# First attention with deeper probability slots, other quotient, square and rotary steps; two gate tiles moved; matmuls placed in waits

## The chip, the cores and the metric

The kernel runs on one core of one Trainium2 chip. The metric is the time of one execution in device microseconds (us). A core has a matmul engine (TensorE, PE in the profile; its weight loads are PEld), a vector engine (VectorE, DVE), an activation engine (ScalarE, ACT), GpSimd (POOL), a queue engine for transfers (SyncE, SP), a large on-chip memory (SBUF) and the matmuls' accumulators (PSUM, eight banks of 512 columns).

## What is computed

Two different two-layer blocks, one after the other, on a sequence of 512 rows of width 1024, in float32. A layer of the first block mixes three attentions behind one input projection:

```
proj = rms_norm(x, attn_norm[l]) @ w_in[l]
o_mla  = rms_norm(mla_attention(h_mla, ...), mla_out_norm[l])      # 6 heads, rotary on 32 of 96 columns
o_diff = diff_attention(h_diff, ...)                               # 6 heads, a = softmax_0 - lam * softmax_1, then rms_norm
o_ch   = rms_norm(chunk_attention(h_ch, ...), chunk_out_norm[l])   # 4 heads, relative bias
x = x + concatenate([o_mla, o_diff, o_ch]) @ w_out[l]
x = x + conv_ffn(rms_norm(x, ffn_norm[l]), ...)                    # width 2816, three-tap convolution
```

A layer of the second block has a banded attention (8 heads) and three dilated ones (12 heads) whose outputs are combined by their softmax denominators, two sigmoid gates, a projection, a layer norm, a squared-relu network of width 4096 with a gated extra term, and another layer norm:

```
ob = sum over g of softmax(lse)[g] * outs[g]
h = (sigmoid(gate_a) * (oa @ w_branch_a) + sigmoid(gate_b) * (ob @ w_branch_b)) @ w_out
x = layer_norm(alpha * x + h);  x = layer_norm(alpha * x + mlp(x) + ple(x))
```

## The kernel before, in words

Activations lie transposed, 128 of the 1024 features by 512 rows in a chunk. Every float32 weight is split into a high half and a remainder, and so is every activation: a product is three matmuls (L513, L514, L515) in the fast float32 form. A dense tile is 8 chunks by 3 matmuls, 24 in all. Weights come as 460 units of 128x1024. POOL issues the load of a unit's high half (L481) once PE has used up the slot, and then subtracts (L486, two SBUF inputs) to get the remainder. The tiles' PSUM banks go round a ring, banks 2 and 3 alone during the attentions, and `d_free` tells PE that a bank has been read.

**First attention** (`attention_1`, 64 tasks a layer). A task is one head and one block of 128 query rows. Diff tasks have two score maps, the others one. Tasks 0 to 7 are diff, 8 to 15 chunk, 16 to 31 diff, 32 to 55 mla, 56 to 63 chunk. PE's iteration `it` issues the score matmuls of task it+1 (L691; three PSUM banks go round, so the second map of a diff task waits for the reduction of the first map of the task before), then a piece of other work (`fill`: quarters of dense tiles up to iteration 23, from 24 to 36 the mla's small products), then the transposes of task it-2 (L704) and the value matmuls of task it-3 (L714). DVE's iteration `it` reduces the scores of task it to negated logits and a minimum (L1075), after a wait until the transposes of the slot's last user are done: six slots go round by map, so that for diff tasks the last user is three tasks back. Then it forms the quotient of the two denominators of task it-1 (L1085, L1086) and the difference of the maps (L1088), the reciprocal that scales the output (L1090), scales the output of task it-4 out of PSUM (L1095, `on_ready`: frees the bank for PE's L704), squares and sums the output of task it-5 (L1102, both inputs in SBUF), and runs `side(it)`: evacuation of finished dense tiles (L1062), norm factors, and the rotary step of one tile, four dependent instructions (L1206 to L1209). ACT takes the exponentials (L1640), copies transposed probabilities to SBUF (L1647) and evacuates.

After the attention the outputs are scaled by their norm factors, turned into chunks (L727) and split.

**Second attention** (`attention`, 80 tasks). PE's fill is 12 rotary tiles and 12 gate tiles in 96 quarters, spread over the 80 iterations by `pieces`. Then the rows of minima and denominators are turned (L921), 4 more gate tiles run while DVE forms the combination's weights, the weights are spread over partitions by six matmuls whose moving operand has four rows (L930), DVE combines (L1500 to L1502), and PE waits for the last split chunk of the result (L934) before the branch products.

**Norms behind a row.** `factor_from_row` (L869) waits for ACT's root of a row (L1609), turns the row into columns (L874), waits for DVE's reciprocal (L1406) and spreads the factor (L576). PE then waits for the first split chunk of the normalized activations. It runs once after the first block and once in each of the four layer norms, the last of which ends the kernel. In the residual before the first of them DVE sums the squares in `rx`, in SBUF (L1015, L1018).

## Time and profile before

| | |
|---|---|
| median of 3 runs (range) | 3231.89 us (3230.84 to 3237.18) |
| the profiled execution | 3240.42 us, span 3238.7 us |
| mean granted TensorE clock | 0.964 of 2.4 GHz |
| PE busy | 3112.6 us, 96% of the span |
| DVE, ACT, POOL busy | 41%, 25%, 42% |
| first attention, layer 0 and 1 | 60.8 to 306.4 us, 771.3 to 1011.9 us |
| second attention, layer 0 and 1 | 1510 to 1772 us, 2408 to 2670 us |

A timeline row gives start, duration, engine, line, operation, output and inputs, and in brackets how long the engine had been idle and who released it. Several matmul instructions in one row are given as xN; a plain float32 matmul counts as two. Matmuls are pipelined, so the time from start to start is their price, not the duration of one. The granted clock of a stretch is 1.00 at 2.4 GHz and 0.50 at 1.2 GHz.

### The profile page before, as it was taken

The page shows a single profiled execution, that of the slowest core. Times are in us where ns is not written, and L with a number is a line of the kernel's source. Part 1 is how long each engine was busy: PE and PEld are TensorE (multiplying, and loading weights), DVE is VectorE, ACT ScalarE, POOL GpSimd, SP SyncE. Part 2 cuts the span into 40 slices and gives each one's busy share as a digit, 9 for nine tenths or more (in the row PEclk, how much of TensorE's full clock was granted, in tenths as well). Part 3 has the DMA queues.
Part 4 walks back from the last instruction along what each step waited for, and adds up shares of the span by engine and source line. Part 5 has one row for each costly group of instructions (what it writes and reads, how often), then busy time and mean ns, then how long its engine had stood idle before and what let it go on. Part 6 is the DMA issues. An engine that isn't in the chain of part 4 may idle for free.

```text
span 3238.7 us, 40314 instructions
## 1 busy us (share of the span) xinstructions
PE 3112.6 (96%) x13950; PEld 2448.0 (76%) x13950; DVE 1324.1 (41%) x2953; ACT 809.4 (25%) x1811; POOL 1363.7 (42%) x924
## 2 busy tenths in 40 slices
PE   7989999999899999999999999999999999999998
PEld 6767788888667788878666778888686667788886
DVE  5476434244574534353630741112337307411113
ACT  3345212122244212121333221101213333210112
POOL 4211555564211555554222445555352234455552
PEclk9888999999879999999999999999999999999999
DMA  6211566664222566655233556566452235456663
GB/s 239 91 53 53 183 194 194 192 214 153 91 65 79 180 194 187 201 177 176 84 97 112 158 167 193 189 189 202 130 182 91 89 113 157 155 189 189 206 192 102
DMA packets 136518, 494.06 MB, mean 153 GB/s; under 512 B 15280, under 2 KB 15536, under 8 KB 136112
## 3 DMA queue, kind: packets, MB, share of 16 engines
q0 software_dynamic: 66240, 241.20, 24.2%
q1 hardware_dynamic: 68544, 245.40, 23.3%
q10 hardware_dynamic: 1584, 5.40, 0.5%
q8 instruction: 102, 1.67, 0.2%
q14 instruction: 48, 0.39, 0.0%
HBM read 489.84 MB, written 2.10 MB: 152 GB/s over the span
## 4 chain that ended last, share of the span: by engine, by line
PE 91%; DVE 4%; issue 2%; ACT 1%; DMA 1%; POOL 0%; DVEq 0%; SPq 0%; POOLq 0%; ACTq 0%
PE ps L513 25%; PE ps L514 24%; PE ps L515 24%; PE ps L744 3%; PE ps L769 3%; PE ps L691 3%; PE ps L714 2%; PE ps L640 1%; PE ps L641 1%; PE ps L642 1%; PE ps L704 1%; PE ps L757 1%; PE ps L902 1%; DVE small L1086 1%; PE ps L921 0%
## 5 line engine op out<-in xcount | busy, mean ns | idle before, releaser
L513 PE MATMUL ps<-hi,w_hi 128*128 128x512 f32 x3216 | 1294.1, 402 | 34.2 <-POOL w_lo L486 15.2
L514 PE MATMUL ps<-hi,w_lo 128*128 128x512 f32 x3216 | 1268.1, 394 | 0.0
L515 PE MATMUL ps<-lo,w_hi 128*128 128x512 f32 x3216 | 1266.7, 394 | 0.0
L486 POOL TENSOR_TENSOR w_lo<-w_raw,w_hi 128x1024 fp32r<-128x1024 f32 x460 | 1105.8, 2404 | 104.8 <-DMA w_hi<-weights 95.3
L481 POOL DMA_DIRECT2D w_hi<-weights x460 | 261.4, 568 | 1728.2 <-PE ps L515 1573.6
L513 PEld LDWEIGHTS ps<-hi,w_hi 128*128 128x128 f32 x3216 | 612.5, 190 | 233.6 <-issue 94.9
L515 PEld LDWEIGHTS ps<-lo,w_hi 128*128 128x128 f32 x3216 | 612.9, 191 | 131.7
L514 PEld LDWEIGHTS ps<-hi,w_lo 128*128 128x128 f32 x3216 | 613.8, 191 | 121.0
L1120 DVE CUSTOM_DVE_ANT_0 pr<-ps,kc 128x128 f32<-128x128 f32 (+2 forms) x160 | 65.3, 408 | 340.8 <-PE ps L744 340.8
L1803 ACT ACTIVATE ps<-hb,col 128x512 f32<-128x512 f32 x88 | 68.5, 782 | 381.1 <-DVE hb L1062 381.1
L1538 DVE SCALAR_TENSOR_TENSOR x<-x,ps 128x512 f32<-128x512 f32 x64 | 43.9, 687 | 287.1 <-PE ps L515 287.1
L1898 ACT ACTIVATE sq<-ps 128x512 f32<-128x512 f32 x64 | 38.2, 597 | 469.4 <-PE ps L515 469.4
L1671 ACT ACTIVATE pT<-ps 128x128 f32<-128x128 f32 (+2 forms) x160 | 59.8, 374 | 311.6 <-PE ps L757 311.6
L1215 DVE TENSOR_TENSOR x<-x,ps 128x512 f32<-128x512 f32 x64 | 43.8, 687 | 227.5 <-PE ps L515 227.5
L1062 DVE TENSOR_TENSOR hb<-ps,rx 128x512 f32<-128x512 f32 x88 | 60.1, 686 | 187.3 <-PE ps L515 174.3
L1532 DVE SCALAR_TENSOR_TENSOR ps<-ps,sq 128x512 f32<-128x512 f32 x64 | 44.7, 698 | 216.5 <-ACT sq L1898 147.4
L993 DVE TENSOR_TENSOR lo<-ps,hi 128x512 fp32r<-128x512 f32 x108 | 74.7, 692 | 77.1 <-ACT hi L1571 77.1
L769 PE MATMUL ps<-pT,v 128*64 128x128 f32 x608 | 100.7, 286 | 0.3
L640 PE MATMUL ps<-w_hi,hi 128*128 128x384 f32 (+2 forms) x256 | 87.3, 341 | 2.7 <-issue 2.0
L769 PEld LDWEIGHTS ps<-pT,v 128*64 128x64 f32 x608 | 62.0, 136 | 34.3 <-issue 33.1
L1571 ACT ACTIVATE hi<-ps 128x512 fp32r<-128x512 f32 x108 | 64.7, 599 | 88.0 <-DVE ps L1532 54.5
L642 PE MATMUL ps<-w_hi,lo 128*128 128x384 f32 (+2 forms) x256 | 86.4, 337 | 0.0
(317 smaller groups left out, 3235.5 us busy)
## 6 DMA issues: line engine op xcount, KB each, us to landing
w_raw<-weights SPq DMA_DIRECT2D x460, 512.0 KB, 3.8
w_hi<-weights POOLq DMA_DIRECT2D x460, 512.0 KB, 4.5
x<-xt SPq DMA_DIRECT2D x8, 256.0 KB, 10.4
out<-x SPq DMA_DIRECT2D x8, 256.0 KB, 2.1
kc<-k ACTq DMA_DIRECT2D x1, 1281.0 KB, 5.8
bias<-relb ACTq DMA_DIRECT2D x2, 512.0 KB, 5.4
bias<-relb ACTq DMA_DIRECT2D x1, 1024.0 KB, 5.0
praw<-pt ACTq DMA_DIRECT2D x2, 512.0 KB, 3.6
```

The source lines that it names most:

```text
L481: pool.dma_start(whi[s][:, :], weights[i * RING + s]).then_inc(w_hi_in[s], 16)
L486: nc.gpsimd.tensor_tensor(wlo[s][:, :], raw[s][:, :], whi[s][:, :].bitcast(F32), ALU.subtract).then_inc(w_split, 1)
L513: nc.tensor.matmul(out_ap, w[0], xx[0], start=first, stop=False)
L514: nc.tensor.matmul(out_ap, w[1], xx[0], start=False, stop=False)
L515: return nc.tensor.matmul(out_ap, w[0], xx[1], start=False, stop=last)
L640: nc.tensor.matmul(o, xh, whi[slot][:, w], start=(u == 0 and k == 0), stop=False)
L642: last = nc.tensor.matmul(o, xl, whi[slot][:, w], start=False, stop=(u == n_units - 1 and k == per - 1))
L691: nc.tensor.matmul(ps[:, S_BANK[q.s % 3], 0:t.n], lq, rk, start=True, stop=True).then_inc(s_done, 1)
L744: nc.tensor.matmul(ps[:, S_BANK[q.s % 3], 0:t.n], lq, rk, start=True, stop=True).then_inc(s_done, 1)
L769: last = nc.tensor.matmul(ps[t.base:t.base + 64, O_BANK, t.qb * P:(t.qb + 1) * P], v, slots(it - 3)[1][t.id % 2][:, kb * P:(kb + 1) * P], ...
L993: V.tensor_tensor(dst[1][:, i, :], src, dst[0][:, i, :].bitcast(F32), ALU.subtract).then_inc(lo_ready, 1)
L1803: A_(cv[k], hb[k][:, 2:S + 2], ACT.Identity, bias=pcol("conv", l, 3 * 44 + j), scale=pcol("conv", l, 2 * 44 + j)).then_inc(act_step, 1)
```

## The change

In the first attention a probability map goes to slot `task % 4`, the second map of a diff task to slot 4 or 5. DVE's reduction waits for the transposes of the task four back, or, for a second map, for its own difference two diff tasks back. The scale of the quotient becomes a tensor_scalar with two per-row scalars. The reciprocals are kept in a tile of 64 columns. The square pass reads the unscaled output in PSUM and the scaled one in SBUF, writes its product to PSUM, runs in the same iteration as the scaling (with a wait between them), and `on_ready` now follows it; the missing factor is put in by one multiplication before the norm factors. The rotary step of a tile is cut in two, the second half one iteration later. In the last residual of the first block the squares are summed in PSUM. In the second attention two gate tiles leave the fill (88 quarters) and stand behind L930. `keep_busy` adds plain float32 matmuls of 512 columns into bank 2: three at the start, two before PE's wait for the row's root and two after the spread of the factor.

```diff
-                            if s - 6 in SLOT_TASK:
-                                dve.wait_ge(t_done, SLOT_TASK[s - 6] + 1)
+                            if m:
+                                if q.pair >= 2:
+                                    dve.wait_ge(p_ready, t.p0 - 1)
+                                q.pair += 1
+                            elif it >= 4:
+                                dve.wait_ge(t_done, t.id - 3)
...
-                            link(V.scalar_tensor_tensor(out=quot(s), in0=quot(s + 1), scalar=lam, in1=rsum(s), op0=ALU.mult,
-                                                        op1=ALU.mult))
-                            V.scalar_tensor_tensor(out=p0, in0=pb[(s + 1) % 6][:, 0:t.n], scalar=quot(s), in1=p0,
+                            link(V.tensor_scalar(quot(s), quot(s + 1), lam, rsum(s), ALU.mult, ALU.mult))
+                            V.scalar_tensor_tensor(out=p0, in0=p1, scalar=quot(s), in1=p0,
                                                    op0=ALU.mult, op1=ALU.add).then_inc(p_ready, 1)
-                        V.reciprocal(rinv(on0 + it - 1), rsum(s)).then_inc(rinv_ready, 1)
...
-                        V.tensor_scalar(t.more["out"], ps[:, TO_BANK[i % 3], 0:64], rinv(on0 + i), None,
-                                        ALU.mult).then_inc(on_ready, 1)
-                    if 0 <= it - 5 < n:
...
-                        V.tensor_tensor_reduce(out=junk[:, :], in0=t.more["out"], in1=t.more["out"], scale=1.0, scalar=0.0,
-                                               op0=ALU.mult, op1=ALU.add, accum_out=t.more["ss"]).then_inc(ss_ready, 1)
+                        link(V.tensor_scalar(t.more["out"], ps[:, TO_BANK[i % 3], 0:64], rinv(t.more["ss"]), None, ALU.mult))
+                    if 1 <= it <= n:
+                        t = ts[it - 1]
+                        V.reciprocal(rinv(t.more["ss"]), rsum(t.s0)).then_inc(rinv_ready, 1)
+                    if 0 <= it - 4 < n:
+                        if on0 + it - 4:
+                            dve.wait_ge(on_ready, on0 + it - 4)
+                        V.tensor_tensor_reduce(out=ps[:, TO_BANK[i % 3], 64:128], in0=ps[:, TO_BANK[i % 3], 0:64], in1=ts[i].more["out"], scale=1.0,
+                                               scalar=0.0, op0=ALU.mult, op1=ALU.add,
+                                               accum_out=ss[:, ts[i].more["ss"]:ts[i].more["ss"] + 1]).then_inc(on_ready, 1)
...
-                to, so_far = (rx[:, :] if n < NC_ or c == n - 1 else acc), (rx[:, :] if n < NC_ else acc)
+                to, so_far = (rx[:, :] if n < NC_ - 1 or c == n - 1 else acc), (rx[:, :] if n < NC_ - 1 else acc)
...
-        N_ROPE, N_GATE, N_CHAIN = 12, 12, 4
+        N_ROPE, N_GATE, N_CHAIN, N_COMBINE = 12, 10, 4, 2
...
+            def keep_busy(n, rows):
+                for _ in range(n):
+                    nc.tensor.matmul(ps[:, 2, :], ident, rows, start=True, stop=True)
+
             pe.wait_ge(par_in, 48)
+            keep_busy(3, kc1[:, 0:S])
...
             def factor_from_row():
+                keep_busy(2, kc2[:, K2["cos"]:K2["cos"] + S])
                 q.root += 1
                 pe.wait_ge(row_rooted, q.root)
...
                 q.norm += 1
+                keep_busy(2, kc2[:, K2["cos"]:K2["cos"] + S])
...
                                          bk[g][0:4, :], start=True, stop=True).then_inc(wbc, 1)
+                quarters(4 * N_COMBINE, A)
                 oneed = q.chunk
...
+                    if it == AT_KR + 1:
+                        rope_96_add(kr)
+                    elif ITEM_AT.get(it - 3, " ")[0] == "Q":
+                        rope_96_add(mq[b][int(ITEM_AT[it - 3][1])])
...
+                        link(V.tensor_tensor(ss[:, 0:48], ss[:, 0:48], rinvs[:, 0:48], ALU.mult))
...
-                for j in range(N_GATE, 2 * NC_):
+                for j in range(N_GATE, N_GATE + N_CHAIN):
                     gate(j)
                 for pair in range(2):
                     q.val += 1
                     act.wait_ge(val_ready, q.val)
                     high(tmp[pair][:, :], (ohi, olo), 4 + pair)
+                    gate(N_GATE + N_CHAIN + pair)
```

## Rows read from the trace of the kernel before

**Rows 1.** The page, part 4: shares by engine of the chain that ended last.

```profile
PE 91%; DVE 4%; issue 2%; ACT 1%; DMA 1%; POOL 0%; DVEq 0%; SPq 0%; POOLq 0%; ACTq 0%
```

**Rows 2.** Windows, attentions: length, busy PE PEld DVE ACT POOL, clock, DMA, GB/s.

```profile
60.84:306.40 245.56, 223.34 (x1041) 167.53 (x1041) 161.95 (x582) 101.55 (x278) 46.05 (x31) 0.86 0.22 71
771.27:1011.90 240.63, 224.04 (x1041) 167.11 (x1041) 152.62 (x572) 98.41 (x274) 45.87 (x31) 0.86 0.24 73
1518.00:1772.00 254.00, 253.87 (x1175) 173.66 (x1173) 107.80 (x339) 86.92 (x287) 69.47 (x48) 1.00 0.30 96
```

**Rows 3.** PE's waits, first attention of layer 0: us in total, times, longest.

```profile
PE ps L691 <- DVE small L1075: 11.6, 5, 4.3
PE ps L576 <- DVE tmp L1062: 2.0, 1, 2.0
```

**Rows 4.** PE's waits, first attention of layer 1, same columns.

```profile
PE ps L691 <- DVE small L1075: 7.5, 5, 2.9
```

**Rows 5.** Timeline of layer 0's first attention: DVE, POOL and PE.

```profile
177.92 0.29 DVE L1075 CUSTOM_DVE_ANT_0 mk<-ps,dist 128x128 f32<-128x128 f32 x1 [3.43 <-PE ps L704]
178.54 2.68 DVE L1086 SCALAR_TENSOR_TENSOR small<-small 128x1 f32<-128x1 f32 x1
178.79 2.41 POOL L486 TENSOR_TENSOR w_lo<-w_raw,w_hi 128x1024 fp32r<-128x1024 f32 x1
...
185.11 0.68 DVE L1209 TENSOR_TENSOR tmp<-tmp,tmp 32x512 f32<-32x512 f32 x1
186.31 1.48 PE L691 MATMUL ps<-dk,dq 32*128 32x384 f32 x2 [2.79 <-DVE small L1075]
```

**Rows 6.** Lines L1086, L1102, L1088, whole run: ns min/median/max, first and last start.

```profile
L1086 DVE SCALAR_TENSOR_TENSOR small<-small x48: 218/220/2901, 64.6 to 944.5; 128x1 f32<-128x1 f32 x48
L1102 DVE CUSTOM_DVE_ANT_0 junk<-vd x48: 211/215/2385, 187.5 to 975.0; 128x64 f32<-128x64 f32 x48
L1088 DVE SCALAR_TENSOR_TENSOR mk<-mk,small,mk x23: 351/484/752, 64.9 to 912.5; 128x128 f32<-128x128 f32 x7, 128x256 f32<-128x256 f32 x6, 128x512 f32<-128x512 f32 x6, 128x384 f32<-128x384 f32 x4
```

**Rows 7.** Timeline of DVE: a square pass in layer 0.

```profile
148.35 2.49 DVE L1102 CUSTOM_DVE_ANT_0 junk<-dq 128x64 f32<-128x64 f32 x1
```

**Rows 8.** Windows behind gaps, columns as Rows 2: one stretch, sum of eight.

```profile
186.80:193.60 6.80, 6.80 (x18) 4.62 (x17) 0.88 (x6) 0.59 (x4) 0.00 (x0) 0.52 0.00 0
...
sum 47.70, PE 46.16 PEld 32.33 DVE 21.46 ACT 9.54 POOL 0.08; mean PE 5.77 PEld 4.04 DVE 2.68 ACT 1.19 POOL 0.01
```

**Rows 9.** Timeline, combination of the second block's layer 0: PE; then the window.

```profile
1803.07 5.91 PE L930 MATMUL ps<-bk,kc 4*128 4x512 f32 x12
1813.08 0.80 PE L513 MATMUL ps<-ohi,w_hi 128*128 128x512 f32 x1 [4.11 <-DVE olo L993]
...
1808.10:1818.30 10.20, 6.09 (x15) 4.11 (x14) 4.69 (x8) 3.69 (x5) 0.00 (x0) 0.51 0.11 45
```

**Rows 10.** Timeline and window, layer norm of the second block's layer 0: PE.

```profile
1896.32 7.03 PE L902 MATMUL ps<-sq,kc 128*1 128x512 f32 x16 [1.51 <-ACT sq L1583]
1904.11 1.05 PE L874 MATMUL ps<-kc,tmp 1*128 1x1 f32 x8 [0.77 <-ACT tmp L1609]
1909.07 0.77 PE L513 MATMUL ps<-hi,w_hi 128*128 128x512 f32 x1 [2.47 <-DVE lo L1440]
...
1907.00:1914.00 7.00, 4.93 (x12) 3.94 (x13) 6.73 (x11) 6.44 (x10) 0.00 (x0) 0.52 0.01 2
```

**Rows 11.** Timeline and windows, norm after the first block: PE; line L1018.

```profile
1432.95 1.05 PE L874 MATMUL ps<-kc,tmp 1*128 1x1 f32 x8 [2.11 <-ACT tmp L1609]
...
1436.00:1443.00 7.00, 5.25 (x13) 4.17 (x14) 6.82 (x11) 3.58 (x6) 0.00 (x0) 0.53 0.00 0
...
L1018 DVE TENSOR_TENSOR rx<-rx,sq x5: 1046/1622/2254, 1411.5 to 1427.8; 128x512 f32<-128x512 f32 x5
```

**Rows 12.** The start: ACT's and PE's first rows, then two windows, PE alone.

```profile
9.91 1.33 ACT L1597 ACTIVATE hi<-x,col 128x512 fp32r<-128x512 f32 x2 [3.97 <-DMA col<-cols]
...
14.97 0.77 PE L513 MATMUL ps<-hi,w_hi 128*128 128x512 f32 x1 [14.97 <-POOL w_lo L486]
...
15.00:19.00 4.00, 4.00 (x10) 1.00 1.04 408
19.00:28.00 9.00, 9.00 (x41) 1.00 0.99 362
```

More of the change, by code:

```diff
@@ L108, in __init__ @@
         self.s = self.task = self.o = self.x = self.rope = self.kcopy = self.bca = self.bcd = self.mu = 0
-        self.sink = self.on = self.chunks = self.root = self.mean = self.back = self.sd = self.var = self.sums = self.aux = self.quarter = 0
+        self.sink = self.on = self.chunks = self.root = self.mean = self.back = self.sd = self.var = self.sums = self.aux = self.quarter = self.pair = 0
     def freed(self, bank):
@@ L253, in build @@
         rsum = lambda s: small[:, 32 + s % 16:33 + s % 16]
-        rinv = lambda s: small[:, 48 + s % 16:49 + s % 16]
+        rinv2 = lambda s: small[:, 48 + s % 16:49 + s % 16]
+        rinv = lambda k: rinvs[:, k:k + 1]
         esk = lambda s: small[:, 64 + s % 16:65 + s % 16]
@@ L364, in tasks_1 @@
                                   0, None, qb, False, False, add=dist[:, off:off + n], after=after,
-                                  out=dn[h // 2][:, qb, 64 * (h % 2):64 * (h % 2) + 64], ss=ss[:, 4 * h + qb:4 * h + qb + 1]))
+                                  out=dn[h // 2][:, qb, 64 * (h % 2):64 * (h % 2) + 64], ss=4 * h + qb))
             for h in range(CH_H):
@@ L384, in tasks_1 @@
                                    out=mn[h // 2][:, qb, 64 * (h % 2):64 * (h % 2) + 64],
-                                   ss=ss[:, 24 + 6 * qb + h:25 + 6 * qb + h], value=tile_1(l, f"V{qb}") if h == 0 else None, **more))
+                                   ss=24 + 6 * qb + h, value=tile_1(l, f"V{qb}") if h == 0 else None, **more))
             return d[0:8] + c_[0:8] + d[8:24] + m_ + c_[8:16]
@@ L704, in attention_1 @@
                             last = nc.tensor.transpose(ps[:, TO_BANK[i % 3], kb * P:(kb + 1) * P],
-                                                       slots(i)[0][t.s0 % 6][:, kb * P:(kb + 1) * P], ident)
+                                                       slots(i)[0][i % 4][:, kb * P:(kb + 1) * P], ident)
                         last.then_inc(t_done, 1)
@@ L1066, in attention_1 @@
                 on0 = q.on
-                for it in range(n + 5):
+                for it in range(n + 4):
                     if it < n:
@@ L1072, in attention_1 @@
                             dve.wait_ge(s_done, s + 1)
[L1073 to L1076 removed]
+                            if m:
[4 more added lines that the diff above has]
+                                dve.wait_ge(t_done, t.id - 3)
+                            V.tensor_tensor_reduce(out=pb[4 + it % 2 if m else it % 4][:, 0:t.n], in0=ps[:, S_BANK[s % 3], 0:t.n],
+                                                   in1=t.more["add"], scale=-t.scale, scalar=3.0e38, op0=ALU.add, op1=ALU.min,
                                                    accum_out=ngm(s)).then_inc(s_free, 1)
@@ L1133, in attention @@
                         p0 = pb[s % 6][:, 0:t.n]
-                        if t.kind == "diff":
-                            V.reciprocal(rinv(s), rsum(s))
-                            link(V.reciprocal(rinv(s + 1), rsum(s + 1)))
-                            V.tensor_scalar(p0, p0, rinv(s), None, ALU.mult)
-                            link(V.tensor_scalar(rinv(s + 1), rinv(s + 1), lam, None, ALU.mult))
-                            V.scalar_tensor_tensor(out=p0, in0=pb[(s + 1) % 6][:, 0:t.n], scalar=rinv(s + 1), in1=p0,
-                                                   op0=ALU.mult, op1=ALU.add).then_inc(p_ready, 1)
-                        elif t.kind in ("norm", "sink"):
-                            if t.kind == "sink":
-                                link(V.tensor_tensor(rsum(s), rsum(s), esk(s), ALU.add))
-                            link(V.reciprocal(rinv(s), rsum(s)))
-                            V.tensor_scalar(p0, p0, rinv(s), None, ALU.mult).then_inc(p_ready, 1)
+                        if t.kind == "sink":
+                            link(V.tensor_tensor(rsum(s), rsum(s), esk(s), ALU.add))
+                            link(V.reciprocal(rinv2(s), rsum(s)))
+                            V.tensor_scalar(p0, p0, rinv2(s), None, ALU.mult).then_inc(p_ready, 1)
                     if side:
@@ L1317, in side @@
                         dve.wait_ge(*landed(name))
-                        rope_96(mq[b][int(name[1])])
+                        rope_96_turn(mq[b][int(name[1])])
                     elif it == AT_FACTOR:
-                        dve.wait_ge(ss_ready, q.on + 56)
+                        dve.wait_ge(on_ready, q.on + 56)
+                        link(V.tensor_tensor(ss[:, 0:48], ss[:, 0:48], rinvs[:, 0:48], ALU.mult))
                         link(V.reduce_sum(ss[:, 24:28], ss[:, 24:48].rearrange("p (q h) -> p q h", q=NTB), axis=AX.X))
@@ L1356, in low_turned @@
                     q.chunk += 1
-                dve.wait_ge(ss_ready, q.on)
+                dve.wait_ge(on_ready, q.on)
+                link(V.tensor_tensor(ss[:, 48:64], ss[:, 48:64], rinvs[:, 48:64], ALU.mult))
                 link(V.reduce_sum(ss[:, 48:52], ss[:, 48:64].rearrange("p (q h) -> p q h", q=NTB), axis=AX.X))
@@ L1474, in _ @@
                 attention(TASKS["2", l], slots_2, side=dilated)
-                q.tile += N_GATE + N_CHAIN
-                q.unit += N_GATE + N_CHAIN
+                q.tile += N_GATE + N_CHAIN + N_COMBINE
+                q.unit += N_GATE + N_CHAIN + N_COMBINE
                 for c in range(4):
```

24 lines of the change are left out of this document (10 added, 14 removed).

## The prediction

> **What bounds the kernel now.** I read the chain of waits first: PE carries 91% of it and DVE 4% [rows 1], so the time is PE's own work, its idle gaps, and the stretches in which it works at half clock. Then the windows, for where that is. The first attention takes 245.6 and 240.6 us, PE is idle for 22 and 17 us of them, and the granted clock is 0.86; the second attention is idle for 0.1 us of 254 at 1.00 [rows 2]. PE's waits in the first attention name mostly one releaser, the score reductions L1075: 11.6 us in layer 0, 7.5 in layer 1, and beside them one wait of 2.0 us in each layer for an evacuation L1062 [rows 3, 4].
>
> The timeline shows how such a gap comes about [rows 5]. DVE idles 3.43 us until PE's transposes free a slot (177.92). Its quotient L1086, 0.22 us in the median, then takes 2.68 us while POOL's subtraction L486 runs. Evacuation and four rotary instructions follow, and PE, whose next score matmul needs the next reduction, idles 2.79 us until 186.31. Then it works at 1.2 GHz: from 186.8 to 193.6 the clock is 0.52 with PE busy throughout [rows 8]. I compared the clock with the gaps one by one: each low stretch of the first attention stands at or just behind a gap of PE. So a gap is paid twice, as idle time and as half-speed work behind it.
>
> **The change, part by part**, against the profiled execution (span 3238.7, its time 3240.4).
>
> *Slots.* For a diff task the wait for transposes goes from three tasks back to four. Three back, it could be met only after PE's fill and transposes of the iteration whose scores are already there. Four back, it is met before those scores are issued. DVE now reduces beside the fill, some 3 us earlier, and that much delay no longer reaches PE. Single-map tasks fall from six slots to four at no cost, by the same order. Behind a second map's new wait nothing is queued that its own difference, two diff tasks back, hasn't passed.
>
> *Quotient and square.* L1086 and L1102 go from 0.22 us to 2.9 and 2.5 when they meet POOL [rows 6, 7]. The new square pass has one SBUF input, and I cost it at the 0.22 us of the old. L1088 still has two SBUF inputs. It never took over 0.75 us [rows 6], but it always stood behind L1086, which had sat out POOL's instruction, so that row doesn't excuse it. I expect that it mostly misses POOL now, because with the new slots the quotient runs beside the fill, and POOL starts when a fill's last quarter frees a unit.
>
> The Trainium skill, "SBUF — State Buffer", section "Who interferes with whom", says that a DVE instruction with two SBUF inputs contends with a GpSimd instruction that reads SBUF, that the one that comes second is blocked for the whole instruction, and that a DVE instruction with at most one SBUF input outside the two-port modes isn't. By that rule L1102's stalls go, while L1086's may only move on to L1088; that result is the second case below. The trace agrees for the two lines that it shows stalled.
>
> *Rotary in halves.* The same four instructions, some 0.7 us each, in two iterations: a block of 2.8 us becomes two of 1.4. The halves end one iteration later, with three or more iterations to go before their tasks.
>
> *What is late next.* In iterations 24 to 36 DVE is as full as PE (diff tasks plus six rotary tiles), so I count nothing there. The 4.3 us gap of layer 0 comes from the rotary angles, a chain of instructions the change doesn't touch. What is open are the gaps 1.27, 2.79, 1.31 and 2.0 us in layer 0 and 1.30, 2.86, 0.94 and 2.0 in layer 1, 14.5 us, and the eight low stretches behind them, in which PE is busy for 46.2 us [rows 8] that full clock would do in half: 23.1. Together 37.6 us. Others that stay (1.3 us for ACT's squares, 0.8 for an evacuation) will keep some stretches low, so I take two thirds, 25. Bounds: 10 (only the two 2.0 us gaps, which a square pass causes, with half of their low stretches' work) and 41.
>
> *Later `on_ready`.* PE's transposes and the turn of the outputs now wait for the square too, about 0.35 us behind the scaling (the square with its accumulator read, 0.30, and the wait). Inside the attention the slack of an iteration hides it. At its end, with one more small multiplication, I charge 0.6 us a layer: -1.2. Attention: **-24**.
>
> *Sums of squares in PSUM.* The last L1018 takes 1.05 us [rows 11] and is waited for; the PSUM form elsewhere takes 0.70. **-0.35**.
>
> *Start.* The parameters are there at 9.9, PE starts at 14.97, and its first ten matmuls take 0.40 us each against 0.22 later [rows 12] (the clock column says 1.00 there, the spacing says half). Three `keep_busy` matmuls at half speed take 3 x 1.76 = 5.3 us and end at 15.2. The ten then save 1.8 us, and the load of the next high half, issued when these tiles end, comes as much earlier: **-1.8** (bounds 0 and -2).
>
> *Norms.* A plain matmul of 512 columns is 7.03/8 = 0.88 us [rows 10], a pair 1.76. In the norm after the first block the wait for the root is 2.11 us [rows 11], so the first pair hides. In the layer norms that wait is 0.77 us [rows 10], and the pair overhangs by 1.0 us, four times. The pair after the spread hides (2.3 to 2.5 us of idle time). What it can bring is the clock: 0.52 for 7 us behind each norm [rows 10, 11]. PE's busy time there is 4.9 and 5.25 us, half of which is the loss, capped by DVE's chunks, which come every 1.4 to 1.5 us: 2.2 us a layer norm, 2.9 the first. I believe in a kept clock at 0.75 for three layer norms and 0.65 for the first: 1.9 + 3 x (1.65 - 1.0) - 1.0 for the last, after which PE has nothing to do = **-3** (bounds +4 and -5.7).
>
> *Two gate tiles.* Each is 24 matmuls at 0.228 us, 5.5. They leave an attention without idle time, which gets shorter by 10.9 us, and stand where PE now idles 4.11 us [rows 9]. They end at about 1819, after DVE's last chunk, which becomes ready at about 1816 since its ACT half is now queued behind a gate evacuation that waits for the first tile. So the 4.1 us go whole; the sigmoids start some 5 us later and have the branch tiles' four banks as cover. The clock is already low as L930 ends, before the gap begins (low from 1808.1), so I don't expect it to stay up: 6.1 us busy at half [rows 9] become 3.4 to 7. I take 4.5 a layer, **-9** (bounds -6 and -13).
>
> Sum: 24 + 0.35 + 1.8 + 3 + 9 = 38.2 us. The profiled execution is 8.5 us above the runs' median; from the median 3231.9 the forecast is **3193.7 us**.
>
> **The rivals.** *Forecast*, 3183 to 3203, chance 0.50.
>
> *The stall moves on.* L1088 meets POOL in L1086's place. For it: its two inputs; against it: the new phase. Attention brings 10 - 1.2, the rest 14.2: 3209. Chance 0.24.
>
> *All gaps close* and every low stretch behind them: attention 40, norms 5.7, gates 13, start 2: 3171. Chance 0.16. Against it: gaps that belong to ACT and to the angles.
>
> *It doesn't do what it says*: DVE, busy for 162 of 246 us [rows 2], finds other waits (for the exponentials, for `pv_done`), the norms cost their 4 us, and the gates' gain is all that is left with it: 3228. Chance 0.06.
>
> *Slower.* The second attention loses 8 of 96 quarters, the densest work in it. If its clock then fell as in the first, from 1.00 to 0.86, each layer would take 254/0.86 - 254 = 41 us more: 3231.9 - 38 + 82 = 3276. It decides from a mean clock of 0.93, where 19 us a layer eat the gain. Against it: already now four of five iterations have one quarter, and none of the stretches between is low. Chance 0.04.
>
> **How the numbers follow.** The likeliest gives 3193.7. From 3172 to 3214 hold all of the forecast, most of the second case and half of the third, 0.8. 0.2% is 6.5 us, about what a measurement can tell. Faster by more: 0.50 + 0.24 + 0.16 and a little of the fourth, 0.91; the same 0.05; slower 0.04.
>
> **What would show it.** PE's waits for L1075 in the first attention under 8 us in both layers together (now 19.1) and its clock above 0.90; no instruction of the square pass above 0.4 us; L1088 at 2.4 us or more would be the second case. No wait of PE before the branch products; gate tiles at 1.2 GHz for part of their time. Between L902 and L874 some 1.8 us instead of 0.77, and full clock behind the norms. PE's first dense matmuls 0.22 us apart. Wrong it would be if the first attention took over 238 us in both layers, or if the second's clock left 1.00.

## The result, and the profile after

The changed kernel takes 3181.24 us (median of 5, 3175.22 to 3236.52); the kernel before, in the same session, 3231.89 (median of 5, 3220.64 to 3237.18). The medians are 50.6 us apart, where 38.2 were forecast. The ratio is 0.9837, with a 95% interval of 0.9816 to 0.9859; it leaves out executions over 1.5% above their kernel's fastest, here the one of 3236.52. A second set of four executions gave 3198.8 (3168.55 to 3236.9) against 3235.61, ratio 0.9888 (0.9834 to 0.9942).

The executions of the changed kernel lie 68 us apart, those of the old one 25. Two of the nine took 3236.52 and 3236.9 us, with mean clocks of 0.958 and 0.960. The first of them was profiled with the result: its clock stays low through the end of both first attentions. The rows below are from an execution of 3168.55 us (span 3166.9, after_again) unless a sentence says otherwise. That is the fastest of the nine, and the profiled execution of the kernel before (3240.42 us) is one of the longer ones: their spans differ by 71.8 us and not by 50.6, so what follows for each part is the gain between these two executions. The difference between the two kinds turned out to be the part of the result that I had not seen coming; tail_kick, below, is about it.

The chain of waits of the changed kernel, shares by engine (before: [rows 1]):

```profile
PE 93%; DVE 3%; issue 1%; ACT 1%; DMA 0%; POOL 0%; ACTq 0%; DVEq 0%; POOLq 0%
```

The two first attentions and a stretch of the second, columns as in [rows 2]:

```profile
58.73:282.39 223.66, 208.12 (x1042) 155.96 (x1042) 152.62 (x589) 100.78 (x278) 46.24 (x31) 0.90 0.25 80
745.28:958.25 212.97, 201.47 (x1041) 151.74 (x1041) 144.81 (x577) 96.98 (x274) 46.16 (x31) 0.93 0.27 84
1461.80:1695.00 233.20, 233.20 (x1086) 158.51 (x1084) 103.31 (x330) 82.12 (x272) 61.87 (x42) 1.00 0.30 92
```

The first attentions are 21.9 and 27.7 us shorter. PE's busy time fell by 15 and 23 us although it does the same matmuls: that is work done at full instead of half clock. The second attention keeps its 1.00, so the slower rival is out.

PE's waits in the first attention of layer 0, then of layer 1 (before: [rows 3, 4]):

```profile
PE ps L692 <- DVE small L1089: 5.2, 2, 4.3
PE ps L514 <- ACT mk L1770: 2.2, 2, 2.0
PE ps L692 <- ACT vc L1644: 1.8, 1, 1.8
...
PE ps L692 <- DVE small L1089: 1.2, 2, 0.9
```

The waits for a reduction (L1089, before L1075) fell from 11.6 and 7.5 us to 5.2 and 1.2. What is left is the 4.3 us of the rotary angles, and a wait for ACT's copy of K2 (L1770), one of the mla's small products.

The lines on DVE that answer to [rows 6]: the difference of the maps L1101, the quotient's scale L1100, the square pass L1114; ns min/median/max:

```profile
L1101 DVE SCALAR_TENSOR_TENSOR mk<-mq,small,mk x34: 352/619/3210, 62.8 to 865.9; 128x128 f32<-128x128 f32 x10, 128x256 f32<-128x256 f32 x8, 128x384 f32<-128x384 f32 x8, 128x512 f32<-128x512 f32 x8
L1100 DVE TENSOR_SCALAR small<-small x48: 272/273/276, 62.5 to 892.1; 128x1 f32<-128x1 f32 x48
L1114 DVE CUSTOM_DVE_ANT_0 ps<-ps,vd x48: 211/214/219, 170.3 to 920.0; 128x64 f32<-128x64 f32 x48
L1114 DVE CUSTOM_DVE_ANT_0 ps<-ps,vm x32: 212/214/233, 244.9 to 943.1; 128x64 f32<-128x64 f32 x32
```

The quotient and the square never stall any more, and not for want of meeting POOL: 4 of the 48 quotients and 18 of the 128 squares begin during one of its subtractions and take no longer than the others. The difference, which before never took over 0.75 us, now does: six of its 48 take over 1 us, two of these 3.21 and 2.77. The stall moved on, but to far fewer places.

The spread of the combination's weights (before: [rows 9]), and a window of the gate tiles:

```profile
1732.45 8.20 PE L939 MATMUL ps<-bk,kc 4*128 4x512 f32 x12
1740.58 0.79 PE L514 MATMUL ps<-hi,w_hi 128*128 128x512 f32 x1
1741.17 0.63 PE L515 MATMUL ps<-hi,w_lo 128*128 128x512 f32 x1
...
1736.00:1746.00 10.00, 10.00 (x20) 5.60 (x19) 5.67 (x9) 0.63 (x1) 0.03 (x1) 0.54 0.17 58
```

The 4.11 us of idle time before the branch products are gone. The first ten matmuls of the moved tiles stand 0.43 us apart, which is half clock; after that 0.23. The spread itself takes 8.20 us in this execution where L930 took 5.91, because the clock falls earlier in it (0.65 over it, before 0.90).

The norm of a layer norm, layer 0 (before: [rows 10]), and the window behind it:

```profile
1834.92 7.03 PE L911 MATMUL ps<-sq,kc 128*1 128x512 f32 x16 [1.51 <-ACT sq L1598]
1841.88 1.99 PE L780 MATMUL ps<-kc,kc 128*128 128x512 f32 x4
1843.79 1.05 PE L882 MATMUL ps<-kc,tmp 1*128 1x1 f32 x8
1845.12 1.16 PE L577 MATMUL ps<-kc,small 128*128 128x128 f32 x8 [0.28 <-DVE small L1421]
1846.11 1.88 PE L780 MATMUL ps<-kc,kc 128*128 128x512 f32 x4
1848.75 0.47 PE L514 MATMUL ps<-hi,w_hi 128*128 128x512 f32 x1 [0.76 <-DVE lo L1455]
...
1849.00:1856.00 7.00, 7.00 (x31) 5.08 (x31) 6.82 (x11) 6.68 (x12) 0.00 (x0) 1.00 0.00 0
```

From the squares' sum (L911) to the turn (L882) it is 8.87 us instead of 7.79 (L902 to L874): the pair overhangs by 1.1. The clock behind is 1.00 instead of 0.52.

The start (before: [rows 12]), PE, then its first window:

```profile
9.98 5.11 PE L780 MATMUL ps<-kc 128*128 128x512 f32 x6 [9.98 <-DMA col<-cols]
14.57 0.75 PE L514 MATMUL ps<-hi,w_hi 128*128 128x512 f32 x1
15.16 0.39 PE L515 MATMUL ps<-hi,w_lo 128*128 128x512 f32 x1
...
15.00:19.00 4.00, 4.00 (x19) 1.00 1.05 409
```

From 15 to 19 us PE starts 19 matmuls instead of 10.

I cut both traces at the same instructions and added up length, PE's idle time and time at half clock, in us:

| part | before | after |
|---|---|---|
| start | 60.8 / 17.4 / 0 | 58.7 / 12.5 / 0 |
| first attention, layer 0, iterations 0 to 23 | 142.6 / 12.5 / 37.5 | 129.0 / 7.2 / 23.9 |
| iterations 24 to 36 | 51.0 / 8.9 / 13.3 | 43.5 / 4.5 / 8.5 |
| iterations 37 to the end | 52.4 / 1.2 / 18.2 | 51.1 / 3.9 / 10.2 |
| layer 1, iterations 0 to 23 | 135.0 / 8.8 / 27.3 | 118.2 / 3.0 / 10.2 |
| iterations 24 to 36 | 52.0 / 6.0 / 20.9 | 43.6 / 4.7 / 8.5 |
| iterations 37 to the end | 53.7 / 1.9 / 19.5 | 51.2 / 3.9 / 10.2 |
| rest of the first block, with its last norm | 962.8 / 23.3 / 20.2 | 958.4 / 17.7 / 13.9 |
| second attention with its branch products, up to the layer norm, layer 0 | 382.4 / 5.5 / 20.4 | 377.6 / 1.5 / 13.6 |
| the same, layer 1 | 382.7 / 5.5 / 20.4 | 372.5 / 1.4 / 3.4 |
| layer norms and networks, four parts (idle time up to PE's last instruction) | 963.2 / 25.7 / 34.8 | 963.1 / 18.0 / 12.1 |

### The profile page after: what moved, and what is told of

Same layout as the page of the kernel before. It is cut to its first block, busy times and chain, and to the rows that moved or that the text cites. A ratio compares the mean times of both kernels' runs of the same rounds, so it can differ in the third digit from the quotient of the medians.

```text
span 3234.8 us, 40285 instructions
## 1 busy us (share of the span) xinstructions
PE 3153.1 (97%) x13996; PEld 2468.6 (76%) x13996; DVE 1305.9 (40%) x2957; ACT 808.3 (25%) x1811; POOL 1363.4 (42%) x924
## 3 DMA queue, kind: packets, MB, share of 16 engines
q1 hardware_dynamic: 68544, 245.40, 23.5%
## 4 chain that ended last, share of the span: by engine, by line
PE 93%; DVE 3%; issue 1%; ACT 1%; DMA 1%; POOL 0%; ACTq 0%; DVEq 0%; POOLq 0%
PE ps L514 25%; PE ps L515 24%; PE ps L516 23%; PE ps L692 3%; PE ps L745 3%; PE ps L770 3%; PE ps L715 3%; PE ps L705 2%; PE ps L641 1%; PE ps L643 1%; PE ps L642 1%; PE ps L758 1%; PE ps L911 1%; DMA w_hi<-weights 1%; PE ps L930 0%
## 5 line engine op out<-in xcount | busy, mean ns | idle before, releaser
L1914 ACT ACTIVATE sq<-ps 128x512 f32<-128x512 f32 x64 | 38.2, 597 | 465.8 <-PE ps L516 465.8
```

## Experiments

Each run's time stands beside the kernel before on the same chip (3233.6 to 3235.6 us). The first four ran together on one chip, the next four on a second, the last four on a third.

**after_again** is the changed kernel itself.

> The changed kernel as it is, for an undisturbed trace: about 3181 us. In the first attention PE's waits for the score reductions fall from 19.1 us in both layers to under 8, the clock rises above 0.90. If instead the stall only moved from the quotient to the difference of the maps, that line shows instructions of 2.4 us and the waits stay above 12 us.

Measured: 3198.8 us, ratio 0.9888 (0.9834 to 0.9942), and the trace above. The gain is there, but four executions from 3168.55 to 3236.9 can't tell a few us. I therefore read the other experiments by their traces' parts first and by medians second.

**old_slots** puts the old wait back and leaves the rest.

```diff
-                            elif it >= 4:
+                            if s - 6 in SLOT_TASK:
+                                dve.wait_ge(t_done, SLOT_TASK[s - 6] + 1)
+                            if not m and it >= 4:
                                 dve.wait_ge(t_done, t.id - 3)
```

> Only the slot wait is put back: a reduction of a diff task waits again for the transposes three tasks back. Theory 1 (the earlier reductions give PE its gain): some 22 us slower than the changed kernel, 3203 us, with waits of PE for the reductions of 10 us or more. Theory 2 (the passes that no longer wait for POOL give it): at most 5 us slower, 3186.

Measured: 3219.3 us, ratio 0.9946 (0.9923 to 0.9970). PE waits 9.6 and 5.8 us for reductions again. That is theory 1, with a time 16 us above the one that it gave. The first attentions take 246.3 and 240.1 us, together 486.4; before it was 486.6. By parts it is less even: iterations 0 to 36 take 187.9 and 177.2 us, 5.7 and 9.8 less than before and 15.4 more than in the changed kernel, in both layers; the end takes 58.4 and 62.9 us, with 20 and 28 of them at half clock, and gives the rest back. So the slots carry 15.4 of the 21.1 and 25.2 us that these iterations gained. The difference L1103 and DVE around one of its stalls, then POOL beside it:

```profile
L1103 DVE SCALAR_TENSOR_TENSOR mk<-mq,small,mk x34: 350/619/3139, 63.1 to 903.0; 128x128 f32<-128x128 f32 x10, 128x256 f32<-128x256 f32 x8, 128x384 f32<-128x384 f32 x8, 128x512 f32<-128x512 f32 x8
...
173.76 0.29 DVE L1091 CUSTOM_DVE_ANT_0 mk<-ps,dist 128x128 f32<-128x128 f32 x1 [3.20 <-issue]
174.39 0.27 DVE L1102 TENSOR_SCALAR small<-small 128x1 f32<-128x1 f32 x1
174.70 2.90 DVE L1103 SCALAR_TENSOR_TENSOR mk<-mq,small,mk 128x512 f32<-128x512 f32 x1
...
174.63 2.41 POOL L487 TENSOR_TENSOR w_lo<-w_raw,w_hi 128x1024 fp32r<-128x1024 f32 x1
```

This is the picture of [rows 5], one instruction later: DVE idles 3.20 us, passes the quotient in 0.27, and the difference sits out POOL's subtraction, which began 0.07 us earlier. It happens to 13 of the 48 differences, 1.8 to 3.1 us each, as it happened to 13 of 48 quotients in the old kernel. The new form of the quotient is not the one that is held up: in this run five quotients begin during a subtraction and take 0.27 us each, where all six that did so in the kernel before took 1.6 to 2.4. The rule of the Trainium skill ("SBUF — State Buffer", section "Who interferes with whom"), that a DVE instruction with two SBUF inputs contends with GpSimd's and that the one that comes second is blocked, is borne out by the line that took the stall over: all 11 differences that begin during a subtraction take 1.8 us or more. Which comes second can't be told by the recorded starts, though: 7 of the 13 quotients stalled in the kernel before began 0.24 to 0.47 us ahead of the subtraction, as the one of [rows 5] did. What takes the stall away is the phase: with the new slots 13 become 6, and of these only two exceed 1.3 us. How much of the 15.4 us is this, and how much the earlier reduction by itself, no run separates.

**old_lock** is the other half: new slots, but the quotient's scale and the square pass with two SBUF inputs as before.

```diff
-                            link(V.tensor_scalar(quot(s), quot(s + 1), lam, rsum(s), ALU.mult, ALU.mult))
+                            link(V.scalar_tensor_tensor(out=quot(s), in0=quot(s + 1), scalar=lam, in1=rsum(s), op0=ALU.mult,
+                                                        op1=ALU.mult))
...
-  in0=ps[:, TO_BANK[i % 3], 0:64], in1=ts[i].more["out"], scale=1.0,
+  in0=ts[i].more["out"], in1=ts[i].more["out"], scale=1.0,
```

> Only the quotient and the square pass read two SBUF inputs again. Theory 1 (slots): the square passes stall again, the two waits of 2.0 us at the spread and the low stretches behind them come back, some 8 us slower, 3189. Theory 2 (POOL's lock): 20 us slower, 3201.

Measured: 3199.32 us (3194.17 to 3201.88), ratio 0.9884 (0.9855 to 0.9914). Quotient, difference and square:

```profile
L1100 DVE SCALAR_TENSOR_TENSOR small<-small x48: 219/220/2681, 62.1 to 917.6; 128x1 f32<-128x1 f32 x48
L1102 DVE SCALAR_TENSOR_TENSOR mk<-mq,small,mk x34: 350/485/753, 62.4 to 891.8; 128x128 f32<-128x128 f32 x10, 128x256 f32<-128x256 f32 x8, 128x384 f32<-128x384 f32 x8, 128x512 f32<-128x512 f32 x8
L1115 DVE CUSTOM_DVE_ANT_0 ps<-vd x48: 213/215/2893, 170.0 to 953.8; 128x64 f32<-128x64 f32 x48
```

The quotient stalls three times (5.1 us together) where it stalled 13 times before. The square, now in the iteration of the scaling, stalls 22 times of 128, 52.7 us together, where it stalled 12 times (26.4 us). PE's wait for an evacuation before a spread, 2.0 us in the kernel before and gone in the changed one, is back too, 2.06 us in each layer, with 6.8 us at half clock behind it. In layer 0:

```profile
PE ps L577 <- DVE tmp L1072: 2.1, 1, 2.1
```

As a time, 3199.32 can't be told from the changed kernel's 3198.8. The first attentions take 239.4 and 232.9 us. In iterations 0 to 36 that is 1.7 and 8.1 us more than in the changed kernel; the rest, 14.1 and 11.8, lies in the end, at half clock for 41 and 36 us. So before the end of the attention the new forms of quotient and square together earn 1.7 and 8.1 us between these traces, of which some may be chance: two executions of the changed kernel differ by 4.6 us in iterations 0 to 23 alone (129.0 and 124.4). Whether the stalls at the end also bring the low clock there, or it was chance, these four executions don't say.

**gates_in_fill** puts the two gate tiles back into the attention.

```diff
-        N_ROPE, N_GATE, N_CHAIN, N_COMBINE = 12, 10, 4, 2
+        N_ROPE, N_GATE, N_CHAIN, N_COMBINE = 12, 12, 4, 0
```

> The two gate tiles go back into the fill of the second attention. Theory 1: PE idles 4.1 us again before the branch products in each layer and the clock stays low longer, 9 us slower, 3190. Rival (the clock is not low any more behind the gates): 13 us slower. Rival (the later sigmoids cost what the idle time gave): within 2 us.

Measured: 3200.21 us (3179.57 to 3217.12), which can't be told from 3198.8. PE's wait before the branch products is back:

```profile
PE ps L514 <- DVE olo L1003: 4.0, 1, 4.0
```

From the start of the second attention to the layer norm it takes 382.8 and 380.7 us. In the changed kernel that part varies by where the low stretches fall, so I took all eleven traces with the tiles moved: layer 0 from 372.6 to 379.1, mean 377.3; layer 1 from 372.5 to 379.7, mean 376.6. The three traces with the tiles in the fill (before, before_kick and this one) have a mean of 381.6. The move is worth 4.2 and 4.9 us, about the idle time it fills and no more.

**tail_kick** asks why executions of the same kernel lie 68 us apart. I compared the part from the end of the 2.0-us wait for K2 to the end of the attention. First the long execution (3236.5 us), then the short (3168.55), both layers each:

```profile
226.80:308.82 82.02, 80.60 (x280) 61.38 (x279) 39.93 (x192) 32.30 (x90) 8.25 (x5) 0.50 0.15 49
936.70:1018.83 82.13, 79.54 (x281) 60.94 (x281) 39.90 (x193) 32.43 (x91) 8.51 (x6) 0.52 0.15 49
...
231.10:282.39 51.29, 47.42 (x283) 37.11 (x282) 38.51 (x193) 32.35 (x91) 8.53 (x6) 0.90 0.24 79
906.98:958.25 51.27, 47.41 (x282) 37.09 (x281) 38.36 (x193) 32.31 (x91) 8.48 (x6) 0.90 0.23 79
```

The same matmuls, 82 us against 51: 61.6 of the 68 us between the two spans lie here. The engine that does the work isn't waiting (PE busy 80.6 of 82.0); in layer 0 it runs at 1.2 GHz from the wait on, to the end of the attention. In layer 1 the low clock that lasts doesn't begin behind the wait for K2. There the clock comes back, and falls for good at PE's next gap, in iteration 38, where PE waits for an exponential (L1655):

```profile
934.79 0.42 PE L514 MATMUL ps<-w_hi,mhi 128*128 128x384 f32 x1 [1.96 <-ACT mk L1770]
941.62 0.31 PE L705 MATMUL ps<-kc,pr 128*128 128x128 f32 x1 [1.01 <-ACT pr L1655]
...
935.70:939.10 3.40, 3.40 (x15) 2.69 (x13) 3.30 (x8) 1.37 (x4) 2.88 (x3) 0.50 0.50 148
939.10:942.50 3.40, 1.81 (x8) 0.82 (x7) 3.27 (x15) 1.58 (x5) 3.13 (x3) 1.00 0.67 213
942.60:1018.80 76.20, 75.25 (x265) 58.33 (x265) 34.14 (x175) 29.68 (x83) 2.90 (x3) 0.50 0.11 36
```

So it is in layer 1 of gates_in_fill and of no_root_pair, where a low stretch of 37.5 us begins at the same gap and the end takes 69.1 and 69.5 us. The short execution has the same gap (1.15 us) with no low clock behind it. The experiment puts four plain matmuls of 512 columns, from here on the kick, into iteration 39, just behind this gap, all else as in the changed kernel.

```diff
                     elif it in ITEM_AT:
                         item(ITEM_AT[it])
+                    elif it == 39:
+                        for bk_ in (2, 3):
+                            pe.wait_ge(d_free[bk_], q.freed(bk_))
+                        keep_busy(4, kc1[:, 0:S])
```

> The changed kernel with four plain matmuls of 512 columns at iteration 39 of each first attention, behind the wait for the last small product. Theory 1 (a low clock that begins with PE's last gap there outlasts the iterations without fill in some executions, and this makes the slow ones): the four cost 3.5 us a layer at full clock, the slow executions of 3199 us and more go, the spread between runs halves, the median falls to some 3178. Theory 2 (the clock of that part has nothing to do with what PE is given there): 7 us slower and as wide a spread.

Measured: 3185.0 us (3183.33 to 3190.05, five executions), ratio 0.9843 (0.9826 to 0.9861). The added matmuls and the same part of both layers:

```profile
238.94 3.60 PE L780 MATMUL ps<-kc 128*128 128x512 f32 x8
...
231.80:286.53 54.73, 50.93 (x290) 38.68 (x289) 38.68 (x192) 32.16 (x91) 8.50 (x6) 0.91 0.23 74
910.90:968.63 57.73, 53.58 (x290) 39.98 (x290) 38.29 (x192) 32.14 (x91) 8.54 (x6) 0.85 0.21 70
```

It costs 3.4 and 6.5 us against the short execution and saves 27 and 24 against the long one. With the kick, in this and three later kernels, 19 executions lie between 3178.2 and 3193.4. Without it 11 of 27 were over 3200 (five kernels: this one as it is, gates_in_fill, values_swapped, no_root_pair, rotary_whole); on the chip of tail_kick itself 5 of 14. The spread is what theory 1 said; the median is not, it stays at 3185.0 where some 3178 were expected.

**before_kick** asks whether the old kernel pays for the same thing: the same insertion in the kernel before.

> The kernel before, with the four plain matmuls of the run tail_kick (iteration 39 of each first attention, behind a wait for banks 2 and 3). Question: does the old kernel also lose time to a low clock in the iterations without fill? In its trace the low stretch behind the 2.0-us gap ended after 13.7 us of PE's work, in the changed kernel's slower executions it lasted 85 to 92 us. Theory A, the long low stretch belongs to the changed kernel alone (its tail is as dense as before, but PE has fewer gaps in front of it): the kick has nothing to remove, costs up to 2 x 3.5 us (four matmuls of 0.88 us) less what the gap hides, and the time is 3234 to 3243 beside the kernel before's 3235.6. Theory B, the old kernel pays for it in part of its executions as well: the time is 3215 to 3230, and part of what tail_kick brought isn't the change's.

Measured: 3235.54 us (3229.72 to 3250.65, 12 executions) against 3233.64, ratio 1.0017 (1.0001 to 1.0032). As a time the kick only costs. In its trace the two ends do get shorter, 51.2 and 51.3 us with 5.3 and 5.8 at half clock, where the old kernel's trace has 52.4 and 53.7 with 18.2 and 19.5, but not by enough to pay for it. Two ends of 82 us fit none of the old kernel's executions, which all lie within 25 us. So the long low stretch is new with the change.

What in the change lets it last is not shown. The work is the same, and nearly the same wait stands in front (2.2 us before, 2.0 after). One thing differs: the old kernel has no gap over 0.5 us between that wait and iteration 62, in either trace, and the changed one has those of iteration 38, 1.0 to 1.2 us and 0.6 behind it, in three of the four ends of its two traces. No run tests them alone. rotary_whole, below, has none of them and no execution over 3193.56, which would fit, but it is four executions; and in layer 0 of the long execution the low clock began before iteration 38.

**values_swapped** moves the wait for K2, by computing V2 ahead of it.

```diff
-"Q4", "Q5", "K2", "V2", "V3"]
+"Q4", "Q5", "V2", "K2", "V3"]
```

> The last two small products before the iterations without fill are V2 and K2 in the other order, so that V3 waits for a bank whose evacuation is one ACT instruction and not two. Theory: PE's gap of 2.0 us there shrinks below 1 and the low stretch behind it is shorter, 4 to 10 us in the median. Rival (the gap only moves to another product): within 3 us.

Measured: 3208.69 us (3171.65 to 3237.48), ratio 0.9898 (0.9860 to 0.9936). In its trace iterations 24 to 36 take 42.4 instead of 43.5 us, but the end 55.2 instead of 51.1: the wait shrank to 1.1 us, and the gap in iteration 38 grew to 1.67. Inconclusive as a time, and a no for the idea.

**rotary_whole** does the four rotary instructions in one iteration again.

```diff
-V.tensor_tensor(tmp[2][R, :], tmp[2][R, :], sin1[R, :], ALU.mult).then_inc(rope_turned, 1)
+V.tensor_tensor(tmp[2][R, :], tmp[2][R, :], sin1[R, :], ALU.mult)
+                link(V.tensor_tensor(t[R, :], t[R, :], cos1[R, :], ALU.mult))
+                V.tensor_tensor(t[R, :], t[R, :], tmp[2][R, :], ALU.add).then_inc(rope_done, 1)
```

> Only the rotary step is one piece again. Theory (the earlier reductions already cover the block of 2.8 us): within 4 us of the changed kernel, PE's waits for reductions longer by at most 2 us. Rival (the halves matter): such waits of 1.4 us and more come back at the rotary iterations, with low clock behind them, 10 us slower.

Measured: 3180.82 us (3177.76 to 3193.56), ratio 0.9846 (0.9820 to 0.9871), the lowest median of all. In the trace iterations 24 to 36 take 46.4 us instead of 43.5, and the end 48.9 instead of 51.1. The wait that the rival named does come back, 2.24 and 2.35 us in iteration 29, with low clock, and PE waits 7.5 and 3.4 us for reductions instead of 5.2 and 1.2. In return the gap in iteration 38 is gone. The halves shift 2.9 us out of one part and 2.2 us come back in the next: this piece of the change is worth nothing measurable.

**no_root_pair** leaves out the pair before the root in the four layer norms.

```diff
-                keep_busy(2, kc2[:, K2["cos"]:K2["cos"] + S])
+                if q.root == 0:
+                    keep_busy(2, kc2[:, K2["cos"]:K2["cos"] + S])
                 q.root += 1
```

> The pair of matmuls before the wait for the row's root is left out in the four layer norms and kept in the first norm. Theory: the root's columns (L874 of before) come 1.0 us earlier in each of the four, the clock behind the norms stays at 2.4 GHz thanks to the other pair, 4 us faster, 3177. Rival (both pairs are needed): the stretches at 1.2 GHz behind three norms come back, 2 us slower or equal.

Measured: 3189.32 us (3169.29 to 3210.10), ratio 0.9856 (0.9811 to 0.9900). Layer-norm parts: 422.2, 88.9, 423.1, 24.5 us against 423.2, 89.1, 423.6, 27.2. The pair costs something in each norm and most in the last, where PE has no work behind it; how much there is uncertain, since that part lies between 24.6 and 27.2 us in the traces that have the pair.

**kick_no_pair** is the same on top of the kick, where executions agree better.

> The changed kernel with the tail_kick matmuls and without the pair before the root in the four layer norms (kept in the norm after the first block). In the stage table of no_root_pair against the changed kernel: ln.0a 422.2 against 423.2, ln.0b 88.9 against 89.1, ln.1a 423.1 against 423.6, ln.1b 24.5 against 27.2. If the pair overhangs its wait by 1.0 us each time, as predicted, and brings no clock: 3185.0 - 4 = 3181. If it only costs at the kernel's end: 3182.5. If the clock behind the norms needs the pair: 3186 to 3190, with the 7-us stretches at half clock back.

Measured: 3184.33 us (3179.35 to 3192.49), ratio 0.9857 (0.9835 to 0.9878). Its layer-norm parts, 422.4, 90.3, 422.5, 23.5, are 5.3 us shorter than tail_kick's (423.2, 90.3, 423.6, 26.9), and the two long ones spend 3.4 and 0 us at half clock, where tail_kick's spend none. In the three runs without the pair three of the six long parts have 3.4 to 3.8 us at half clock, in the traces with both pairs none has over 0.3. So the clock needs this pair a little, and less than the pair costs. The medians show 0.7 of it and the ratios the opposite, both less than this measurement can tell.

**kick_no_keep** drops every `keep_busy` of the change and keeps the kick.

> The changed kernel with the tail_kick matmuls, but without all keep_busy matmuls of the change (three at the start, the pairs before the root and behind the spread of the factor in five norms). Price of keep_busy by itself, without the low stretches that blur the other comparisons; beside tail_kick, 3185.0 (3183.3 to 3190.1). Theory A, as predicted: start 1.8 and norms 3 us are lost: 3190. Theory B, the stage table is right (start -2.1, norm after the first block -2.0, layer norms -0.6, -1.2, -0.1 and +3, the last at the kernel's end): some 3 us are lost net: 3188. Theory C, the matmuls behind the spread are worth more than the table shows, since the 7-us stretches at half clock come back in all five norms: 3193 to 3197.

Measured: 3185.23 us (3178.16 to 3193.39), ratio 0.9853 (0.9831 to 0.9875). A window behind the layer norm, layer 0:

```profile
1865.00:1872.00 7.00, 5.08 (x12) 4.04 (x13) 6.73 (x11) 6.51 (x11) 0.00 (x0) 0.58 0.00 0
```

The low clock is back, behind all four norms that dense work follows. The parts against tail_kick: start +1.9, norm after the first block +3.3, layer norms +1.3, +1.7, +1.2, and -2.2 in the last. Together 7.2 us by the traces; the medians show 0.2 and the ratios 0.001, some 3 us, so as a time its worth is not settled.

**kick_swap** is kick_no_pair with the swapped values, meant to be the fastest.

> A version meant to be the fastest: kick_no_pair and in both first attentions V2 before K2 among the small products, so that V3 doesn't wait 2.0 us for ACT's copy of K2. In values_swapped the gap became 1.7 us at another place and the undisturbed profile was 3170.0. If that gap and the low stretch behind it go: two times 1.5 to 4 us less than kick_no_pair, 3173 to 3179. If the wait only moves: the same as kick_no_pair within 2 us. If the new order makes K2 late for its own users: slower by 2 to 5 us.

Measured: 3184.39 us (3179.95 to 3189.82), ratio 0.9858 (0.9835 to 0.9880). The wait only moved. No version beats the changed kernel's median by more than can be measured; the kicked ones differ from it in that they never take 3200.

## Why the prediction was right, and where its terms were not

*Total.* Forecast 3193.7, range 3172 to 3214, measured 3181.24 and, in the second set, 3198.8. Outside the attention 14.2 us were forecast, and the parts give 13.2 (start 2.1, norm 2.0, gates 9.1, layer norms about 0). The attention's 24 were too low: the median of all nine executions, 3187.8, is 45.8 us under the old kernel's 3233.6, and less the 13.2 that leaves some 32 for it, an estimate. That the total came so near is partly luck, since two misses work against each other: a gain that was counted as nothing, and a loss that no case of mine had. The 6.5 us that I gave as what a measurement can tell was too small as well: two medians of the same kernel lie 17.6 us apart.

*Attention, -24.* Measured -50 from trace to trace (486.6 to 436.6). By the table above the gain is 13.6 and 16.8 us in iterations 0 to 23, 30.4 for the 25 that I took mostly for them (of the eight gaps in my list two, 1.31 and 0.94 us, stand in iteration 25). The step that failed is "In iterations 24 to 36 DVE is as full as PE (diff tasks plus six rotary tiles), so I count nothing there": 7.5 and 8.4 us came from there, with the slots above all (old_slots: 52.3 and 49.5 us in these iterations against 43.5). PE had been idle there for 8.9 and 6.0 us before. My list passed over a gap of 1.92 us in iteration 29 of each layer, though the waits of 11.6 and 7.5 us [rows 3, 4] contain it, and in layer 0 gaps of 1.78 and 0.94 us for which the profile names no releaser. The end of the attention gained 1.3 and 2.5 where I had charged 0.6 each.

The mechanism stands: the wait for the slot was the main cause (old_slots loses 15.4 us a layer before the end), and a gap was paid twice. In iterations 0 to 23 PE's idle time fell by 5.3 and 5.8 us and its time at half clock by 13.6 and 17.1, half of which is gain; that makes 12.1 and 14.3 of the 13.6 and 16.8. Not every execution gets as much as this trace: the low clock at the end takes up to 31 us a layer.

*Stall moves on.* Chance 0.24, with L1088 at 2.4 us as its sign. The sign came (3.21 and 2.77 us), the result did not: two of 48 places over 1.3 us. I took the sign for the case; the count would have been the better sign. My reason for expecting a miss, the new phase, is what old_slots confirms.

*Start, -1.8.* Measured -2.1. *Norm after the first block with the sums in PSUM, -1.9 and -0.35.* Measured -2.0 (81.3 to 79.3 us).

*Layer norms, together about -1.* Measured -0.6, -2.4, -0.1 and +3.0, near zero. The -2.4 is not the change's: the same part takes 88.9 us in before_kick, without the pairs, and 89.1 here. The kept clock came behind all four norms that have dense work behind them, so the 0.75 was too careful. The overhang was as costed, 1.1 us. The last norm cost more than the 1.0 that I had charged. The 3.0 of this trace contain 1.7 that the sum of squares lost to a low clock before the pair (8.74 us instead of 7.03); the mean over the eight traces with all pairs is 2.0. No dense work follows there that a kept clock could serve.

*Gates, -9.* Measured -9.1 by the means over eleven traces, -15 in this one, where two low stretches fell away that the tiles have nothing to do with. The clock didn't stay up, as expected.

*Signs.* Waits for the reduction 6.4 us in both layers (under 8), clock 0.90 and 0.93, square pass at most 0.233, no wait before the branch products, 1.00 behind the norms, second attention at 1.00: these came as announced. But "Wrong it would be if the first attention took over 238 us in both layers" also came, in the execution that was profiled with the result: 250.4 and 245.8 us, of which 82.4 and 82.3 in the end. In its iterations 0 to 36 it is as fast as the short one (168.0 and 163.4 us against 172.5 and 161.8). The sign took the whole attention, the change works in its first part.

## What to carry to other kernels

Where two engines block each other, see what stands behind the instruction that you rewrite. The quotient's new operands only handed its stall to the difference, the next instruction with two SBUF inputs; the square's took its stalls away, and no other line took them over. Moving the group in time, by a buffer that comes free an iteration earlier, took away 11 of 13 long ones. Count PE's idle time in every part of a loop before writing "nothing there". And judge a kernel whose executions spread by parts of its trace: here 30 us of work a layer hung on whether the clock came back after gaps of 1 to 2 us, and with four matmuls of 0.9 us placed behind them that loss was not seen again, for some 5 us a layer.

## What the runs showed of the hardware

PE can be busy almost without a break and stay at 1.2 GHz: for 82 us in the end of the first attention in layer 0 (busy 80.6), and for 76 us in layer 1 (busy 75.3), in an execution whose instructions are those of one that takes 51 us there. The work in it is small float32 matmuls of 64 to 512 columns. With four plain matmuls of 128 rows and 512 columns among them, none of 19 executions took over 3193.4 us. The old kernel has the same work there, and its 43 executions all lie between 3220.6 and 3245.4 us. What lets the low clock last in the one and not in the other is open; the gap in iteration 38 is the first thing to test.

VectorE's quotient of 128x1 with two SBUF inputs took 1.6 to 2.4 us each time that it began during GpSimd's subtraction (6 of 6), and 0.27 us as a tensor_scalar with two per-row scalars (5 of 5 in old_slots, 4 of 4 in the changed kernel).
